# One wide one-hot product per token in place of three accumulated ones, for the third block of expert gates

## The reference, cut to what matters

```python
s = einsum('thpc,hpkc->thpk', q, sub_keys)          # 8 heads x 2 halves x 128 keys
sv, si = top_k(s, 16)                                # best 16 keys of each half
cand = sv[:, :, 0, :, None] + sv[:, :, 1, None, :]
best, pos = top_k(cand.reshape(n_tok, 8, 256), 16)   # best 16 pairs of each head
eidx = i * 128 + j of each pick                      # 128 experts of 16384 for a token
g = softmax(best)
act = gelu(einsum('ted,td->te', u_tab[eidx], x))
out = einsum('te,ted->td', g * act, v_tab[eidx])
```

## Time and profile before

| | us |
|---|---|
| median of 3 runs | 2059.49 (2059.1 to 2060.64) |
| the profiled execution, by the same clock | 2061.06 |
| its span, from the first to the last instruction | 2059.2 |
| PE busy in it | 2011.5 (98%) |
| DVE busy in it | 1544.0 (75%) |
| mean granted TensorE clock | 0.993 of full speed |

### The profile page before, as it was taken

How to read it: one execution, slowest core, us unless ns; L and a number is a source line. 1 busy time by engine, 2 the same in 40 slices (tenths; PEclk the granted TensorE clock), 3 DMA queues, 4 the chain that set the end, 5 groups by cost and what they waited for, 6 DMA issues and landing times.

```text
span 2059.2 us, 37564 instructions
## 1 busy us (share of the span) xinstructions
PE 2011.5 (98%) x14922; PEld 1852.2 (90%) x14922; DVE 1544.0 (75%) x2886; ACT 959.6 (47%) x1642; POOL 784.4 (38%) x502
## 2 busy tenths in 40 slices
PE   8999999999999999999998999999999999999998
PEld 7899999999889988887897999999998899888886
DVE  7868996555676578878699879975556766679886
ACT  5654453434444444444655654443434434444443
POOL 1014027777730055642110050088787400456420
PEclk9999999999999999999999999999999999999999
DMA  6684556676765568996422444566667655578973
GB/s 224 211 315 152 168 160 152 156 150 151 183 184 163 178 197 271 329 340 222 133 92 69 128 134 153 174 150 149 157 151 171 182 171 177 190 265 295 326 257 102
DMA packets 165918, 387.68 MB, mean 188 GB/s; under 512 B 55920, under 2 KB 78704, under 8 KB 163440
## 3 DMA queue, kind: packets, MB, share of 16 engines
q1 hardware_dynamic: 113712, 332.58, 49.4%
q0 software_dynamic: 49152, 33.75, 10.4%
q10 hardware_dynamic: 2880, 18.96, 2.3%
HBM read 361.67 MB, written 23.54 MB: 187 GB/s over the span
## 4 chain that ended last, share of the span: by engine, by line
PE 81%; DVE 14%; issue 2%; DMA 2%; ACT 2%; SPq 0%; DVEq 0%; ACTq 0%
PE ps L942 15%; PE ps L944 14%; PE ps L943 14%; PE ps L973 11%; PE ps L975 10%; PE ps L974 10%; PE ps L1020 4%; DVE w_lo L1534 2%; DMA land<-stream_dram 2%; DVE work L1420 2%; ACT w_hi L632 1%; DVE hidden L1420 1%; DVE hidden L1555 0%; DVE hidden L1546 0%; DVE work L1428 0%
## 5 line engine op out<-in xcount | busy, mean ns | idle before, releaser
L1534 DVE TENSOR_TENSOR w_lo<-land,w_hi 128x1024 fp32r<-128x1024 f32 x562 | 686.1, 1221 | 357.1 <-ACT w_hi L632 356.0
L942 PE MATMUL ps<-act_hi,w_hi 128*128 128x288 f32 x2688 | 808.6, 301 | 13.6 <-DVE act_lo L1260 4.8
L632 ACT CAST w_hi<-land 128x1024 fp32r<-128x1024 f32 x592 | 621.5, 1050 | 419.6 <-PE ps L975 299.5
L943 PE MATMUL ps<-act_hi,w_lo 128*128 128x288 f32 x2688 | 795.2, 296 | 0.0
L944 PE MATMUL ps<-act_lo,w_hi 128*128 128x288 f32 x2688 | 792.3, 295 | 0.0
L548 POOL DMA_INDIRECT gates_d<-rstd x256 | 452.6, 1768 | 320.1 <-DVE rstd L1687 193.4
L942 PEld LDWEIGHTS ps<-act_hi,w_hi 128*128 128x128 f32 x2688 | 506.0, 188 | 20.1 <-issue 8.9
L944 PEld LDWEIGHTS ps<-act_lo,w_hi 128*128 128x128 f32 x2688 | 508.1, 189 | 0.0
L943 PEld LDWEIGHTS ps<-act_hi,w_lo 128*128 128x128 f32 x2688 | 507.1, 189 | 1.0
L973 PE MATMUL ps<-w_hi,g_hi 128*128 128x512 f32 x1024 | 403.3, 394 | 5.7 <-DVE g_lo L1839 5.7
L974 PE MATMUL ps<-w_lo,g_hi 128*128 128x512 f32 x1024 | 399.7, 390 | 0.0
(11 more groups left out here) (223 smaller groups left out, 1497.0 us busy)
## 6 DMA issues: line engine op xcount, KB each, us to landing
land<-stream_dram SPq DMA_DIRECT2D x592, 512.0 KB
gates_d<-hidden ACTq DMA_DIRECT2D x16, 1024.0 KB, 5.9
work<-gates_d SPq DMA_DIRECT2D x96, 128.0 KB, 4.5
act_d<-smp_stage SPq DMA_DIRECT2D x64, 64.0 KB
gates_d<-rstd POOLq DMA_INDIRECT x256
hidden<-stream_dram,smp_idx POOLq DMA_INDIRECT x128, 5.9
x<-x_dram SPq DMA_DIRECT2D x4, 288.0 KB, 5.2
y_t_dram<-hidden SPq DMA_DIRECT2D x8, 144.0 KB, 1.9
```

Source lines behind the costliest of these rows:

```text
L632: nc.scalar.copy(w_hi[:, m, :], land[:, n % LANDS, :]).then_inc(w_hi_ready, 1)
L942: nc.tensor.matmul(out, w_hi[:, slot, wsl], hi, start=start, stop=False)
L943: nc.tensor.matmul(out, w_lo[:, slot, wsl], hi, start=False, stop=False)
L1534: V.tensor_tensor(w_lo[:, k, :], land[:, n % LANDS, :], w_hi[:, k, :].bitcast(F32), ALU.subtract).then_inc(lo_by_dve, 1)
```

## The change

Only the third block's chunks change, 8 in each layer. `expand_last` multiplies, for each of the 16 tokens, the token's `j` by all three terms at once: one matmul with 96 moving columns that writes 96 columns of PSUM. The 16 results fill 384 columns in each of banks 0 to 3, four tokens in a bank. Banks 0 and 1 belong to the U slabs before, so the first chunk waits for the last of these to be evacuated, and since all four banks are written by each chunk, PE now waits until the chunk before has been applied. `apply` gains a DVE instruction: a `tensor_reduce` adds up the three terms out of PSUM into the free 128 columns of each bank, `settle()` waits for it, and the product with `hidden` reads the sums. The other two blocks stay as they are.

```diff
+        def all_terms(b, buf):
+            base, tok, n = 2 * (C, B)[buf], GTOK[b], BLOCKS[b][1] - BLOCKS[b][0]
+            return view(work_b, base + tok * (KEYS + n), TERMS, tok // 2, n, 2)
...
+        def last_bank(t):
+            n = BLOCKS[2][1] - BLOCKS[2][0]
+            at = t % 4 * TERMS * n
+            return ps[:, LIN + t // 4, at:at + TERMS * n]
+
+        def last_parts():
+            n = BLOCKS[2][1] - BLOCKS[2][0]
+            banks = ps[:, LIN:LIN + 4, 0:4 * TERMS * n]
+            return banks.rearrange("p b (t k i) -> p b t i k", t=4, k=TERMS)
+
+        def last_sum():
+            n = BLOCKS[2][1] - BLOCKS[2][0]
+            banks = ps[:, LIN:LIN + 4, 4 * TERMS * n:4 * TERMS * n + 4 * n]
+            return banks.rearrange("p b (t i) -> p b t i", t=4)
...
+            def expand_last(L, c):
+                g = GATES * L + GATE0[2] + c
+                pe.wait_ge(onehots_ready, g + 1)
+                pe.wait_ge(gated, g)
+                for k in range(2):
+                    pe.wait_ge(evacuated[k], (L + 1) * USES)
+                j, mask, terms = onehot_views(2, g % 2)
+                for t in range(GTOK[2]):
+                    mm = nc.tensor.matmul(last_bank(t).rearrange("p (k i) -> p k i", k=TERMS), of_token(j, t),
+                                          all_terms(2, g % 2)[:, :, t // 2, :, t % 2], start=True, stop=True)
+                mm.then_inc(expanded, 1)
+
             def expand(L, b, c):
+                if b == 2:
+                    expand_last(L, c)
+                    return
...
+                if b == 2:
+                    did(V.tensor_reduce(last_sum(), last_parts(), AX_X, ALU.add))
+                    settle()
+                    four = tok.rearrange("p i (b t) -> p i b t", b=4)
+                    V.tensor_tensor(four, last_sum().rearrange("p b t i -> p i b t"),
+                                    tok.rearrange("p i (b t) -> p i b t", b=4), ALU.mult).then_inc(gated, 1)
+                    return
                 V.tensor_tensor(tok, ps[:, GBANK + g % 2, 0:GTOK[b] * (hi - lo)].rearrange(
                     "p (t i) -> p i t", t=GTOK[b]), tok, ALU.mult).then_inc(gated, 1)
```

More of the change, by code:

```diff
@@ L245, in view @@
             v = base[:, lo:lo + n]
-            names = "abcd"[:len(dims)]
+            names = "abcde"[:len(dims)]
             if len(dims) > 1:
```

## The result

The changed kernel takes 2074.47 us (median of 5 executions, 2068.06 to 2077.96), the kernel before, beside it, 2059.52 us (median of 5, 2059.1 to 2064.09): 1.0062 times as long, 95% interval 1.0049 to 1.0076, or some 13 to 15 us. The prediction was 2069.3 us with a range up to 2077.5. The profiled execution of the changed kernel is the slowest of its five, 2077.96 us with a span of 2075.9; the spans of the two profiles differ by 16.7 us.

The account below looks back on a forecast made before the run. PE, busy for 98% of the span, was taken as the bound, with DVE bounding at V slab pairs behind a chunk's `apply`. +3.5 us a layer, +7.0 for both, plus 2.8 of clock gave +9.8: 2069.3 us, range 2061.5 to 2077.5.

Parts of the forecast that it names:

- chunk 5: Third block, applied in an even step: the next `g_lo` is one step further on, added DVE time just hidden, -0.51 us.
- chunks 6 and 7: Slabs 232 and 236 start late behind `g_lo`: +0.36 us at the first, +2.95 us in all (2.05 with lower value).
- chunk 8: Slab 242's pair already waited for DVE, so the whole added 1.78 us is lost.
- PE's saving: Third block's expands: 16 matmuls of 96 columns take 0.70 us in place of 1.21, saving 0.51 us a chunk.
- Rival (c): A 96-column matmul costs as much as three of 32, so PE saves nothing: 2074 us, chance 0.04.
- The reduction: On DVE in `apply`: 1536 floats reduced to 512 in 1.75 us, with `settle()` 1.78 us more a chunk.
- Rival (a): The cover holds; with a reduction at two elements a cycle DVE pays 0.9 us: faster, 2056 us, chance 0.07.
- Chunks 2 and 3: `g_lo` stands right behind `apply`, so slab 208 starts late: +0.16 us each, the saving gone.
- DVE's load: DVE over 97% busy from 800 us until slab 242, a sign that the forecast is right.
- The clock: Half clock behind two of four waits, before slabs 236 and 242 in both layers, 1.4 us each: +2.8 us (0 to 6.8).
- Given back: A later wait, such as the 3.62 us one at 931 us, would have taken up the waits if time stayed unchanged.
- Rival (b): Loads don't follow DVE, no clock lost, reduction adds 1.4 us or less: about +1 us a layer, 2061 us, chance 0.09.

Follow-up runs that it names:

- second run: The changed kernel, unaltered, timed and profiled a second time against the kernel before: 2071.85 us, ratio 1.0047.

## Why the prediction was right, and where it was short

The direction, the mechanism and the range held; the point was 5 us too low. In the second run the changed kernel is 10.1 us over the kernel before, where 9.8 were forecast. That this is so close is luck in part: in its profiled execution block and clock make 14.4 us, and slab 270 gives some 4 us back, which the sum had put at nothing. In the table the first column of numbers is the prediction's. The others tell by how much the changed kernel falls back over each chunk, in us, from the slab starts of the two PE timelines (slab 242 of layer 0: 858.12 - 851.25 = 6.87 late, slab 236: 837.82 - 832.84 = 4.98, so +1.89 for chunk 8), with the half clock taken out.

| | predicted | layer 0 | layer 1 | second profile, 0 and 1 |
|---|---|---|---|---|
| chunk 1 | -0.51 | -0.53 | -0.52 | -0.52, -0.52 |
| chunk 2 | +0.16 | +0.35 | +0.34 | +0.35, +0.33 |
| chunk 3 | +0.16 | +0.30 | +0.29 | +0.29, +0.28 |
| chunk 4 | -0.51 | -0.53 | -0.52 | -0.53, -0.53 |
| chunk 5 | -0.51 | +1.13 | +0.54 | +0.60, -0.35 |
| chunks 6 and 7 | +2.95 | +3.00 | +4.01 | +3.87, +3.34 |
| chunk 8 | +1.78 | +1.89 | +1.36 | +1.92, +1.45 |
| a layer | +3.5 | +5.6 | +5.5 | +6.0, +4.0 |
| half clock, a layer | +1.4 | +2.75 | +3.35 | +2.8, +1.6 |

- **PE's saving**: 0.70 us a chunk expected, 0.69 measured; 16 distances of 43 ns. The Trainium skill, "TensorE: Matmul & The Clock Gate", section "Back-to-back issue gap", has two figures: some 81 ns for a stream of pairs at 128 columns, and for a matmul by itself columns / 2.4 + 2.5 ns, an estimate of 42.5 ns for 96. The trace agrees with the second and not with the first. Rival (c), whose 2074 us are nearest to the time measured, is wrong all the same: the kernel without the reduction shows PE's gain in full.
- **The reduction**: 1.75 + 0.03 us expected, 1.761 and 0.03 to 0.04 measured (the 0.02 us put on for PSUM rested on no row). The runs of three cost nothing extra: (1761 - 1226) / 512 = 1.04 ns an element, where the earlier trace rows gave 1.03. The Trainium skill, "VectorE: DVE Perf Modes", section "The perf-mode tier table", gives a reduction the same mode, 1x, in every placement. The trace agrees: 1.04 ns an element out of PSUM, 1.03 out of SBUF. Rival (a) stood on a faster reduction and falls.
- **Chunks 2 and 3**: the end of `g_lo` was foreseen to 0.02 us (750.06, and 750.88 - 0.80 of shift in DVE's queue = 750.08). What was missed is 0.11 to 0.13 us behind each of these waits, where the second matmul starts 0.31 us after the first (751.33 - 751.02) instead of 0.23, and 0.08 us at slab 204, ahead of chunk 2.
- **Chunk 5 is the step that failed.** "The one-hots are built as before, and no DMA is added or moved" is true of the code and false of the time. The prediction named the coupling (reduction, `w_lo`, slab load, cast) at the seventh chunk and did not follow it from the fourth chunk's `apply` to the next loads. There it cost 0.2 to 1.6 us a layer against what was expected.
- **Chunks 6 and 7** were sized at the low end, 2.95 against 3.0 to 4.0 us, for the same reason: late one-hots ahead of the sixth and the seventh chunk. That 2.95 meets the 3.00 of layer 0 is luck in part: chunk 6 was put at 0.36 and came to 0.9 to 2.2 us, chunk 7 at 2.59 and came to 1.8 to 2.3. **Chunk 8** is as predicted, 2.92 us of wait against 2.9.
- **DVE's load**: 96% busy from 802 us to slab 242 (53.87 of 56 us), not over 97%; the rest is the idle time for casts.
- **The clock**: two of four waits were expected to be followed by half clock, and three were (two of four in the second profile). The price was sized too low: 2.75 us behind slab 242's wait in layer 0 (2.8 in the second profile), 1.6 to 1.7 for each of the others, against 1.4. (The high end's own terms, 11.8 and 6.8, make 18.6 us and not 18.)
- **Given back**: the prediction's last sentence named the wait at 931 us as one that might take up what is late. It took up part: slab 270 waits 2.40 us in place of 3.62 and without half clock behind it, 3.9 us. But the kernel without the reduction, which comes to it 1.5 us earlier than the kernel before, waits less there too, so some of the 3.9 us belongs to the one profiled execution of before.
- **Rival (b)**, balance: it fails on all that it asked for, as the loads follow DVE (chunk 5), the clock falls, and the reduction adds 1.79 us. The balance point was misjudged: 1.26 us of added DVE time is already 0.30% slower.

## To carry to other kernels

An operation added to an in-order queue costs what stands behind it: find the next producer that the bounding engine waits for, and put the new work behind it; with four chunks that was worth 5 us for the same work, 3 of them at the two pairs just behind. Then follow the delay a second round, through the buffer that the late instruction frees and the load that it holds up, at every place where it is added and not only where the engine looks full. And move work off the bound only in the stretch where the receiving engine has idle time: with the work behind `g_lo`, the first four chunks gained 0.24%, and all eight gained nothing (a loss of 0.09%, interval from -0.01 to +0.18).

## What the runs showed of the hardware

- The length of a wait does not settle what the granted clock does behind it. Behind waits of 2.92 us ahead of slab 242 it was 0.50 to 0.52 in all four cases (two profiles, two layers), behind 2.07 us ahead of slab 236 once 0.71 and three times 1.00. Behind nearly the same wait ahead of slab 242 it was 0.53 with the reduction alone and 1.00 with the shorter one:

```profile
859.39 0.52 PE L973 MATMUL ps<-w_hi,g_hi 128*128 128x512 f32 x1 [2.37 <-DVE g_lo L1844]
...
859.50:862.90 3.40, 3.40 (x9) 2.70 (x10) 3.40 (x4) 0.00 (x0) 0.57 (x1) 0.53 0.82 265
```

```profile
854.90 0.47 PE L992 MATMUL ps<-w_hi,g_hi 128*128 128x512 f32 x1 [2.39 <-DVE g_lo L1880]
...
855.00:858.40 3.40, 3.40 (x15) 2.80 (x16) 3.40 (x4) 0.40 (x1) 1.71 (x1) 1.00 0.76 235
```

- What else decides it is open; an experiment on the clock alone was not tried.
- The same load of 512 KB, issued as late in each of the four layers of the changed kernel (0.88 to 0.90 us), took from 5.4 to 6.8 us to its cast, in a stretch in which the DMA engines' share is 0.96 (first profile, layer 0).
